# Attention values weighed per key head, with the high and low parts of the values side by side in the stationary block

## The reference

```python
scores = jnp.einsum('bnqhgd,bnkhd->bnhgqk', qb, kk) * (HEAD_DIM ** -0.5)
scores = jnp.where(mask, scores, min)              # band of 128 keys: block before and own block
probs = jax.nn.softmax(jnp.concatenate([scores, sink], -1), -1)[..., :-1]
out = jnp.einsum('bnhgqk,bnkhd->bnqhgd', probs, vv)
...
merged = gate_pool * branch_pool + gate_attn * (out @ w_attn_out)
h = h + merged @ w_out
```

## Time and profile before

| | |
|---|---|
| median of 3 runs | 1046.19 us (1045.76 to 1047.04) |
| the profiled execution | 1046.41 us, its span 1044.6 us |
| TensorE busy | 1037.9 us, 99% of the span |
| VectorE, ScalarE, GpSimd busy | 645.6, 469.7 and 407.3 us |
| granted TensorE clock | 1.000 |
| chain that ended last | PE 95%, DVE 2%, DMA 1% |

### The profile page before, as it was taken

How to read it: one execution, slowest core, us unless ns; L and a number is a source line. 1 busy time by engine, 2 the same in 40 slices (tenths; PEclk the granted TensorE clock), 3 DMA queues, 4 the chain that set the end, 5 groups by cost and what they waited for, 6 DMA issues and landing times.

```text
span 1044.6 us, 15189 instructions
## 1 busy us (share of the span) xinstructions
PE 1037.9 (99%) x5934; PEld 905.1 (87%) x5934; DVE 645.6 (62%) x995; ACT 469.7 (45%) x810; POOL 407.3 (39%) x229
## 2 busy tenths in 40 slices
PE   9999999999999999999999999999999999999998
PEld 7888999998888888888777788888899999988887
DVE  6997776569240377426677656679996776594101
ACT  6443555455231334247676643434345555453210
POOL 1302333325444443344455545434424233254441
PEclk9999999999999999999999999999999999999999
DMA  6735577613232442222111123325367577232232
GB/s 212 216 102 133 162 188 190 186 46 124 94 101 101 141 123 77 89 85 81 61 61 60 51 72 99 101 83 149 111 164 191 155 187 189 85 110 93 101 101 101
DMA packets 42148, 124.81 MB, mean 119 GB/s; under 512 B 4320, under 2 KB 5344, under 8 KB 42080
## 3 DMA queue, kind: packets, MB, share of 16 engines
q1 hardware_dynamic: 37616, 107.89, 31.4%
q0 software_dynamic: 4320, 15.73, 8.8%
q10 hardware_dynamic: 144, 0.26, 0.1%
HBM read 121.76 MB, written 2.10 MB: 119 GB/s over the span
## 4 chain that ended last, share of the span: by engine, by line
PE 95%; DVE 2%; DMA 1%; issue 1%; ACT 1%; SPq 0%; DVEq 0%; ACTq 0%
PE psum L542 21%; PE psum L544 21%; PE psum L543 21%; PE psum L648 9%; PE psum L649 9%; PE psum L650 9%; PE psum L884 1%; PE psum L898 1%; DMA gate_a<-weights_dram 1%; PE psum L792 1%; PE psum L911 1%; DMA w_raw<-weights_dram 1%; PE psum L913 1%; PE psum L912 1%; ACT probs L1352 0%
## 5 line engine op out<-in xcount | busy, mean ns | idle before, releaser
L980 ACT ACTIVATE w_high<-w_raw 128x1024 fp32r<-128x1024 f32 x118 | 124.7, 1056 | 228.8 <-DMA w_raw<-weights_dram 180.9
L1436 POOL TENSOR_TENSOR w_low_in_place<-w_raw,w_high 128x1024 fp32r<-128x1024 f32 x59 | 145.4, 2468 | 177.1 <-ACT w_high L980 176.9
L1436 POOL TENSOR_TENSOR w_low<-w_raw,w_high 128x1024 fp32r<-128x1024 f32 x50 | 122.7, 2457 | 110.3 <-ACT w_high L980 110.3
L542 PE MATMUL psum<-hidden_high,w_high 128*128 128x512 f32 x352 | 137.0, 389 | 0.0
L543 PE MATMUL psum<-hidden_low,w_high 128*128 128x512 f32 x352 | 137.0, 389 | 0.0
L544 PE MATMUL psum<-hidden_high,w_low_in_place 128*128 128x512 f32 x352 | 136.9, 389 | 0.0
L1562 DVE SCALAR_TENSOR_TENSOR h<-psum,h 128x512 f32<-128x512 f32 x24 | 16.5, 690 | 151.0 <-PE psum L544 151.0
L542 PE MATMUL psum<-u_high,w_high 128*128 128x512 f32 x240 | 97.9, 408 | 0.0
L543 PE MATMUL psum<-u_low,w_high 128*128 128x512 f32 x240 | 93.8, 391 | 0.0
L544 PE MATMUL psum<-u_high,w_low 128*128 128x512 f32 x240 | 93.7, 390 | 0.0
L542 PE MATMUL psum<-ffn_u_high,w_high 128*128 128x512 f32 x222 | 87.3, 393 | 0.1
(11 more groups left out here) (262 smaller groups left out, 2812.8 us busy)
## 6 DMA issues: line engine op xcount, KB each, us to landing
w_raw<-weights_dram SPq DMA_DIRECT2D x118, 512.0 KB, 3.5
gate_a<-weights_dram SPq DMA_DIRECT2D x15, 512.0 KB, 6.1
gate_s<-weights_dram SPq DMA_DIRECT2D x15, 512.0 KB, 3.7
gate_s<-weights_dram POOLq DMA_DIRECT2D x15, 512.0 KB, 6.2
up_a<-weights_dram SPq DMA_DIRECT2D x15, 512.0 KB, 4.9
up_s<-weights_dram SPq DMA_DIRECT2D x15, 512.0 KB, 3.6
up_s<-weights_dram POOLq DMA_DIRECT2D x15, 512.0 KB, 8.5
gate_a<-weights_dram SPq DMA_DIRECT2D x15, 256.0 KB, 5.3
```

What stands on the lines that cost most here:

```text
L542: pe.matmul(o, wh, xh, start=start, stop=False)
L980: act.activation(high[:, s, :], raw[:, s, :], ACT.Copy).then_inc(high_done, 1)
L1436: pool.tensor_tensor(wlow[:, s, :], raw[:, s, :], high[:, s, :], ALU.subtract).then_inc(low_done, 1)
```

## The change

The high and low parts of the values go into one stationary block for each key head: `vs[:, k, 0, :]` holds high and low of key head 0, `vs[:, k, 1, :]` low and high of key head 1. One MATMUL of 256 columns then gives the product with the high part in one half of the partitions and that with the low part in the other. `weigh` has four MATMULs of 256 columns per half instead of three of 512, and low x low is now in the sum.

The two halves of the partitions must be joined. ScalarE moves the product with the low part to the other partitions (`small_part`, two copies of 64x256 out of PSUM into `att`), VectorE adds the one with the high part (`attn_add`), ScalarE takes the high part of the sum (`attn_part`, now one copy of 128x256 from SBUF), and VectorE the low part (`attn_part`, one operation of 128x256 from SBUF). This is done one step later than before (`second`, two steps back). The orders of ScalarE's and VectorE's queues change too: VectorE's `attn_add` comes behind `maxima`, `turned_part` behind `pool_gate` and `stage`, `denominators` behind `gate`; ScalarE's `next_unit` goes from before `gate` to the beginning of the next step. The tiles of the first three `U_AO` units are put into another order.

```diff
@@ -233,8 +233,8 @@
         qs_h = put("q_block_high", [P, QT, BLK], m + 16384, F32R)
         ks_h = put("k_block_high", [P, 2 * BLK], m + 20480, F32R)
         ks_l = put("k_block_low", [P, 2 * BLK], m + 21504, F32R)
-        vs_h = put("v_block_high", [P, 2, P], m + 22528, F32R)
-        vs_l = put("v_block_low", [P, 2, P], m + 23552, F32R)
+        vs = put("v_block_parts", [P, 2, KV, P], m + 22528, F32R)
+        att = put("attn_now", [P, 2, BLK], M_GATE_W + 36864)
         smax, msink, smx, nmax, rows, esink, den, rden = [
             put(name, [P, 2, 4], m + 24576 + 32 * i) for i, name in enumerate((
                 "raw_max", "sink_minus_max", "score_max", "neg_max", "row_sums", "exp_sink", "denominator",
@@ -325,6 +325,8 @@
         pt_high = sem("pt_high_done")
         pt_low = sem("pt_low_done")
         weighed = sem("weighed")
+        attn_moved = sem("attn_moved")
+        attn_added = sem("attn_added")
         attn_high = sem("attn_high_done")
         attn_low = sem("attn_low_done")
         gate_scaled = sem("gate_scaled")
@@ -387,9 +389,28 @@
             return (1,) if is_first(nb) else (0, 1)
+        def behind(nb, j, n):
+            if j >= n:
+                return nb, j - n
+            if is_first(nb):
+                return None
+            return nb - 1, j - n + SLOTS
         def turned_count(nb, j):
             return j if is_first(nb) else 8 * nb - 4 + 2 * j
+        def high_parts(k):
+            return vs[:, k, :, :].rearrange("p k v n -> p k (v n)").rearrange("p k (a n) -> p k a n", n=HD)[:, :, 0:4:3, :]
+        def low_parts(k):
+            return vs[:, k, :, :].rearrange("p k v n -> p k (v n)").rearrange("p k (a n) -> p k a n", n=HD)[:, :, 1:3, :]
+        def by_kv(t):
+            return t.rearrange("p k (a n) -> p k a n", n=HD)
         def at(t, k, n=1):
@@ -903,14 +924,17 @@
                 pe.wait_ge(pt_low, turned_count(nb, j) + len(halves(nb)))
-                pe.wait_ge(attn_low, 8 * nb + 2 * j + 1)
+                if not (is_first(nb) and j == 0):
+                    pe.wait_ge(attn_added, 8 * nb + 2 * j)
                 if j == 0:
                     pe.wait_ge(v_block_low, nb + 1)
-                o = psum[:, 0, :]
-                for k in halves(nb):
-                    pe.matmul(o, vs_h[:, k, :], pt_h[:, k, :], start=(k == halves(nb)[0]), stop=False)
-                    pe.matmul(o, vs_h[:, k, :], pt_l[:, k, :], start=False, stop=False)
-                    mm = pe.matmul(o, vs_l[:, k, :], pt_h[:, k, :], start=False, stop=(k == 1))
+                for kv in range(KV):
+                    cols = slice(kv * 2 * BLK, (kv + 1) * 2 * BLK)
+                    for k in halves(nb):
+                        first, last = k == halves(nb)[0], k == 1
+                        pe.matmul(psum[:, 0, cols], vs[:, k, kv, :], pt_h[:, k, cols], start=first, stop=False)
+                        mm = pe.matmul(psum[:, 0, cols], vs[:, k, kv, :], pt_l[:, k, cols], start=False, stop=last)
                 mm.then_inc(weighed, 1)
             def step(nb, j):
@@ -940,17 +964,22 @@
             pe.wait_ge(masked, 16 * NB + 1)
-            pe.wait_ge(attn_low, 8 * NB - 3)
+            pe.wait_ge(attn_low, 4 * NB - 1)
             project(U_AO, 0, 4, oh, ol, tiles=early)
             turn(NB - 1, SLOTS - 1)
             project(U_AO + 1, 1, 5, oh, ol, tiles=early)
             weigh(NB - 1, SLOTS - 1)
-            project(U_AO, 0, 4, oh, ol, tiles=range(TILES // 2, TILES - 2))
-            pe.wait_ge(attn_low, 8 * NB + 1)
-            project(U_AO, 0, 4, oh, ol, tiles=range(TILES - 2, TILES))
-            project(U_AO + 1, 1, 5, oh, ol, tiles=late)
-            project(U_AO + 2, 2, 6, oh, ol)
+            third, fourth = range(TILES // 2, TILES - 2), range(TILES - 2, TILES)
+            pe.wait_ge(attn_low, 4 * NB)
+            project(U_AO, 0, 4, oh, ol, tiles=third)
+            project(U_AO + 1, 1, 5, oh, ol, tiles=third)
+            project(U_AO + 2, 2, 6, oh, ol, tiles=range(TILES - 2))
+            pe.wait_ge(attn_low, 4 * NB + 1)
+            project(U_AO, 0, 4, oh, ol, tiles=fourth)
+            project(U_AO + 1, 1, 5, oh, ol, tiles=fourth)
+            project(U_AO + 2, 2, 6, oh, ol, tiles=fourth)
             project(U_AO + 3, 3, 7, oh, ol)
             for j in range(SLOTS):
@@ -1274,9 +1303,11 @@
                     act.wait_ge(weighed, 4 * nb)
                 if is_first(nb):
-                    act.activation(vs_h[:, 1, :], vtok[:, 1, :], ACT.Copy).then_inc(v_block_high, 1)
+                    act.activation(high_parts(slice(1, 2)), by_kv(vtok[:, 1:2, :]), ACT.Copy
+                                   ).then_inc(v_block_high, 1)
                 else:
-                    act.activation(vs_h[:, :, :], vtok[:, bass.ds(nb, 2), :], ACT.Copy).then_inc(v_block_high, 1)
+                    act.activation(high_parts(slice(0, 2)), by_kv(vtok[:, bass.ds(nb, 2), :]), ACT.Copy
+                                   ).then_inc(v_block_high, 1)
             def pooled_part(g):
                 act.wait_ge(pooled_ready, g + 1)
@@ -1367,28 +1398,38 @@
                 for k in halves(nb):
                     act.activation(pt_h[:, k, :], psum[:, 6 + k, :], ACT.Copy).then_inc(pt_high, 1)
+            def small_part(nb, j):
+                act.wait_ge(weighed, 4 * nb + j + 1)
+                act.wait_ge(attn_low, 4 * nb + j + 1)
+                for kv in range(KV):
+                    r, other = slice(kv * HD, (kv + 1) * HD), slice((1 - kv) * HD, (2 - kv) * HD)
+                    cols = slice(kv * 2 * BLK, (kv + 1) * 2 * BLK)
+                    act.activation(att[r, :, :], psum[other, 0, cols].rearrange("p (a t) -> p a t", a=2), ACT.Copy
+                                   ).then_inc(attn_moved, 1)
             def attn_part(nb, j):
-                act.wait_ge(weighed, 4 * nb + j + 1)
-                for kv in range(KV):
-                    r = slice(kv * HD, (kv + 1) * HD)
-                    act.activation(oh[r, 2 * j:2 * j + 2, bass.ds(nb * BLK, BLK)],
-                                   psum[r, 0, kv * 2 * BLK:(kv + 1) * 2 * BLK].rearrange("p (a t) -> p a t", a=2),
-                                   ACT.Copy).then_inc(attn_high, 1)
+                act.wait_ge(attn_added, 8 * nb + 2 * j + 2)
+                act.activation(oh[:, 2 * j:2 * j + 2, bass.ds(nb * BLK, BLK)], att[:, :, :], ACT.Copy
+                               ).then_inc(attn_high, 1)
             def step(nb, j):
-                before = (nb, j - 1) if j else (nb - 1, SLOTS - 1)
+                before, second = behind(nb, j, 1), behind(nb, j, 2)
                 if j == SLOTS - 1 and not (isinstance(nb, int) and nb == NB - 1):
                     stage_qk(nb + 1)
+                if second is not None:
+                    small_part(*second)
+                next_unit(U_GATE + before[1], before[0])
+                if second is not None:
+                    attn_part(*second)
                 turned_part(*before)
                 exps(nb, j)
-                next_unit(U_GATE + j, nb)
                 gate(nb, j)
-                attn_part(*before)
                 if j == 0:
                     stage_v(nb)
             exps(0, 0)
-            next_unit(U_GATE)
             gate(0, 0)
             for j in range(1, SLOTS):
                 step(0, j)
@@ -1399,7 +1440,11 @@
                 step(nb + 1, 0)
             for j in range(1, SLOTS):
                 step(NB - 1, j)
+            small_part(NB - 1, SLOTS - 2)
+            next_unit(U_GATE + SLOTS - 1, NB - 1)
+            attn_part(NB - 1, SLOTS - 2)
             turned_part(NB - 1, SLOTS - 1)
+            small_part(NB - 1, SLOTS - 1)
             attn_part(NB - 1, SLOTS - 1)
@@ -1489,11 +1534,10 @@
             def stage_v(nb):
                 pool.wait_ge(v_block_high, nb + 1)
                 if is_first(nb):
-                    pool.tensor_tensor(vs_l[:, 1, :], vtok[:, 1, :], vs_h[:, 1, :], ALU.subtract
-                                       ).then_inc(v_block_low, 1)
+                    k, v = slice(1, 2), vtok[:, 1:2, :]
                 else:
-                    pool.tensor_tensor(vs_l[:, :, :], vtok[:, bass.ds(nb, 2), :], vs_h[:, :, :],
-                                       ALU.subtract).then_inc(v_block_low, 1)
+                    k, v = slice(0, 2), vtok[:, bass.ds(nb, 2), :]
+                pool.tensor_tensor(low_parts(k), by_kv(v), high_parts(k), ALU.subtract).then_inc(v_block_low, 1)
             def normalize(nb, j):
                 pool.wait_ge(rden_done, 4 * nb + j + 1)
@@ -2021,14 +2065,18 @@
                     dve.wait_ge(pt_high, turned_count(nb, j) + i + 1)
                     dve.tensor_tensor(pt_l[:, k, :], psum[:, 6 + k, :], pt_h[:, k, :], ALU.subtract).then_inc(pt_low, 1)
+            def attn_add(nb, j):
+                for kv in range(KV):
+                    r, cols = slice(kv * HD, (kv + 1) * HD), slice(kv * 2 * BLK, (kv + 1) * 2 * BLK)
```

(27 more changed lines are left out.)

## The result

| | before | after |
|---|---|---|
| median us | 1045.97 (1045.55 to 1047.04, 4 runs) | 1057.56 (1056.82 to 1058.04, 4 runs) |
| profiled execution, us | 1046.41 | 1057.11 |
| span, us | 1044.6 | 1055.3 |
| first score matmul to start of the last weighing MATMUL, us | 141.71 | 149.00 |
| from there to the end of the span, us | 434.27 | 438.21 |

The ratio is 1.0104, interval 1.0092 to 1.0116. I had 1050.3, with 1041 to 1055. Of the 10.7 us by which the span grew, the attention stage holds 7.3 and everything behind it 3.9; the start of the stage came 0.5 earlier.

A forecast was written before the change was run, and what follows sets the result against it. TensorE, busy 1037.9 of 1044.6 us, was taken as the bound. The terms -5.6 - 1.0 + 4.4 + 1.8 + 0.6 + 3.9 = +4.1 us on the median 1046.19 gave 1050.3 us, range 1041 to 1055.

The forecast's parts named there:

- Weighing: Attention stage, TensorE: fewer columns per MATMUL, 256-column ones 0.12 us apart, save 5.6 us.
- maxima earlier: Attention stage, VectorE: maxima no longer wait for the old step, removing late first steps of blocks 2 and 3; -1.0 us.
- L1991 hits: Attention stage: GpSimd's low part holds VectorE's small L1991 in three of six risky steps, 1.45 us each; +4.4 us.
- The rival with all six hits: Attention stage: L1991 held in all six risky steps, +8.5 us, so 1054.7 us; chance 0.10.
- the one on the clock: Rival, output projection: clock falls behind the `w_out` wait, one unit at half pace, 5.4 us more, 1055.7; chance 0.04.
- My own sign of being wrong: New profile: the prediction is wrong if L1991 stays short, or if the merge's L2089 are not held.
- L1991 is first: Rival, attention stage: L1991 ahead of GpSimd's low part everywhere, merge still late; -0.3 us, so 1045.9; chance 0.20.
- the better rivals: L1991 first everywhere with a late merge (1045.9 us, chance 0.20); neither hit nor late merge (1042.0 us, chance 0.28).
- Fourth step: Attention stage, fourth steps: key staging on VectorE and GpSimd ends later than the next scores want it; +1.8 us.
- `pool_gate` held: Attention stage, second and third steps: GpSimd's low part holds `pool_gate`, low probabilities late in four steps; +0.6 us.
- Late merge: Output projection: new tile order starts VectorE's merge later, TensorE waits for `merged_low` at the first `w_out` unit; +3.9 us.

The follow-up runs named there:

- g2: Changed kernel with GpSimd's key and value staging ahead of its low part, all behind the step's maxima, low part also behind `pool_gate` in second and third steps: 1043.05 us.
- f1: g2 with the output projection order of e1 besides: 1040.12 us, ratio 0.9935 to the kernel before.
- g1: Changed kernel with GpSimd's low part waiting for only the first of the next step's four small VectorE operations: 1058.14 us, ratio 1.0107.
- e4: Changed kernel with GpSimd's low part waiting for all four small VectorE operations of the next step: 1049.73 us, ratio 1.0024.
- f3: Changed kernel with ScalarE's refill (`next_unit`) back behind the exponentials and ahead of the tanh: 1064.58 us, ratio 1.0169.
- e2: Kernel before with only the changed kernel's tile order of the first three output projection units: 1051.06 us, ratio 1.0033.
- e1: Changed kernel with its output projection order half undone, unit 2 whole after the last tiles of units 0 and 1: 1054.68 us, ratio 1.0075.
- f2: e4 with the output projection order of e1: 1045.43 us, ratio 0.9992.
- f4: Kernel before with the changed kernel's weighing, the join in the old place ahead of the maxima, old queue and output projection orders: 1060.49 us, ratio 1.0131.

## Why the prediction was wrong

*Weighing, -5.6 and maxima earlier, -1.0:* right. The stage without its stalls is g2's and f1's: 135.15 us against 141.71, so -6.56 where I had -6.6. The MATMULs are 0.12 apart, as the sum had it.

*L1991 hits, three at 1.45 (+4.4):* this is the step that failed; the hits cost 9.9. I wrote that L1991 is at risk in the first and third steps of blocks 1 to 3, and asked each time only whether it starts ahead of GpSimd. Three more operations follow it, L2038, L2040 and L2041, until T + 3.2, and GpSimd's low part started at T + 2.5 to 3.2. The price of a hit was about right: against 8.42 (7.54 in block 1's first step) the eight hit steps lose 0.97, 1.32, 1.21, 1.62, 1.36, 1.21, 1.05 and, by the late `weigh`, 1.17, together 9.9, a mean of 1.24. Their number was not: all six that I had called at risk, and a second and a fourth step that I had excluded. In the second steps the refill comes later, but the chain lasts longer: the low part at T + 3.20 still met L2041. For the fourth step I had counted on `stage_qk` to delay the refill, but block 3, the last, has no `stage_qk`, and its low part comes at T + 2.97 (4.54 in block 2's). The rival with all six hits (0.10, 1054.7) was the nearest in mechanism; the one on the clock (0.04, 1055.7) was nearer in number, and part of it came as well. My own sign of being wrong, that L1991 stays short, came in all steps of blocks 1 to 3 but one, though the hold was there: the sign watched one operation, as the sum did. g1 shows that protecting L1991 alone is worth nothing, e4 that protecting the four is worth 8.4. So "L1991 is first" was no condition for the better rivals either.

The small operations with two inputs in SBUF were held in the changed kernel and in f3, and the TENSOR_SCALAR with one input as well (2.24 us in the changed kernel). The Trainium skill, page "SBUF — State Buffer", section "SBUF: two separate sides", has a GpSimd operation that started first block VectorE's operations with two SBUF inputs, and those in a two-port mode, for its whole length. For the first kind the traces agree (in f3 L2038 ends at 572.56 and the low part at 572.55). The TENSOR_SCALAR was held in the same way (538.52 and 538.50); in which mode it ran, no row shows. I had stated that rule and then applied it to one operation of four.

*Fourth step, +1.8:* the fourth steps lost 1.33 (block 0), 0.47 and 0.46, so about 2.25, of which 2.0 are the waits for `k_block_low`. Mechanism and size right; in f1 they are gone, with the staging ahead of the low part.

*`pool_gate` held, +0.6:* 0.96 in block 1's second step, 0.24 in block 3's and 0.06 in block 0: 1.3. No run changes this hold alone, but e4, which has it in all six steps, and g2 and f1, where the low part waits for `pool_gated` and these steps last 8.42 to 8.45, agree with the mechanism. Another 0.4 was lost at the last `weigh`, behind a VectorE operation that I had not looked at: L2079, held to 614.78 by the stage's last low part.

*Late merge, +3.9:* the wait was 2.6, at the place forecast. Of its two terms, when `w_out` wants the tile came out at 34.5 us behind the first merge operation (34.35 forecast), and the eighth `merged_low` at 37.1 (38.7 forecast), because the merge's pace is 4.73 us and not 5.0. To the 2.6 comes about 1.7 of half clock in the profiled execution. I had given the fall of the clock a chance of 0.04, as something that a 4 us wait might bring and that costs 5.4; it came with 2.6, and not in every execution: the mean granted clock is 0.998 in the profiles of the changed kernel, e2, e4 and g1, but 1.000 in g2's, which has the same 2.6 us wait. It was 0.998 in three of the changed kernel's four executions and in seven of e2's eight, and at least 0.999 in all of e1, f1 and f2. In e4 the eight executions at 0.997 or 0.998 have a median of 1050.3 us, the two others took 1047.6. Measured by whole runs the late merge costs 2.6 (g2 to f1) to 3.5 us (e2).

Stage by these terms: -6.6 + 9.9 + 2.25 + 1.3 + 0.4 = +7.25, measured +7.3. With the tail's +3.9 and the start's -0.5 it is the measured +10.7. The tail's term came out as forecast partly by luck: a shorter wait, and a half clock that the sum did not have.

Still open is which small operation is caught in a given step. The low part starts within 0.1 us of the end of ScalarE's refill (536.10 and 536.02 in block 2's first step), in the hit steps anywhere from T + 2.48 to T + 3.20, and what moves the refill by these tenths was not followed up. The loss of a hit went from 0.97 to 1.62 us.

## What to carry to other kernels

When an edit brings a row of small VectorE operations near a long GpSimd operation, take the whole row as the target, from the start of its first to the start of its last: protecting the first only hands the hold to the next. Two engines' queues that meet within some tenths of a microsecond should be ordered by a wait, so that the long one starts behind the last of the short ones, and behind the next operation with its inputs in SBUF as well; here that, the staging ahead of the long operation and an earlier merge turned 1% slower into 0.65% faster. Listed waits of the engine that bounds are less than what the holds cost (11.0 against 13.85 us here): compare the lengths of the steps. A step made shorter also takes cover from stalls that were nearly hidden, so a gain on the engine that bounds is to be summed with the slack of each engine behind it.

## What was not expected of the hardware

- A TENSOR_SCALAR on 128x4 elements, one input in SBUF, took 2.24 us beside GpSimd's 2.40 us pass and ended 0.02 behind it; alone it takes 0.17.
- VectorE got one small operation through between two GpSimd operations that follow each other directly (f3: L2038 ends at 572.56, GpSimd's next begins at 572.50 and holds L2040 to 573.27).
- After a 2.6 us wait of TensorE that followed uninterrupted work, the granted clock was 0.50 for some 3.4 us in the changed kernel, beginning about 1.2 us after TensorE had resumed (in e2 and e4 behind the same wait within 0.5), and MATMULs of 512 columns came 0.43 apart. In f3 it fell behind waits of 2.2 and 1.8 us too; in the profile of f4, with a wait of 2.3, it did not. The Trainium skill, page "TensorE: Matmul & The Clock Gate", Part 1, has the clock fall to its lower level after idling; the trace of the changed kernel agrees, and that of g2, with the same wait and no fall, shows that it doesn't always happen.
